# Gated linear attention in a fused transformer kernel: two decay levels written as blocks over the first score products, and a new order of the work around them

## The reference, cut to what matters

```python
def step(state, inp):            # gla_chunk_scan, once forward, once on flipped tokens
    qc, kc, vc, gc = inp
    cum = jnp.cumsum(gc, axis=2)
    o_inter = jnp.einsum('bhcd,bhde->bhce', qc * jnp.exp(cum), state)
    rel = cum[:, :, :, None, :] - cum[:, :, None, :, :]
    decay = jnp.exp(jnp.where(mask[:, :, None], rel, -jnp.inf))
    attn = jnp.einsum('bhid,bhjd,bhijd->bhij', qc, kc, decay)
    o = o_inter + jnp.einsum('bhij,bhje->bhie', attn, vc)
...
k = rmsnorm(dk.reshape(b, n, DIFF_HEADS, 2, DIFF_DH)..., k_norm_g)   # diff_qkv
```

## Time and profile before

| | |
|---|---|
| Median of three runs | 1724.3 us (1721.74 to 1725.12) |
| The profiled execution | 1722.09 us, span 1720.5 us |
| Mean granted TensorE clock | 0.961 |
| TensorE matmuls busy | 1586.4 us |
| VectorE / ScalarE / GpSimd busy | 929.1 / 720.2 / 153.1 us |

### The profile page before, as it was taken

How to read it: one execution, slowest core, us unless ns; L and a number is a source line. 1 busy time by engine, 2 the same in 40 slices (tenths; PEclk the granted TensorE clock), 3 DMA queues, 4 the chain that set the end, 5 groups by cost and what they waited for, 6 DMA issues and landing times.

```text
span 1720.5 us, 18791 instructions
## 1 busy us (share of the span) xinstructions
PE 1586.4 (92%) x7442; PEld 1250.1 (73%) x7442; DVE 929.1 (54%) x1399; ACT 720.2 (42%) x1116; POOL 153.1 (9%) x106
## 2 busy tenths in 40 slices
PE   8998889798989999999899899998876999999995
PEld 1776767587778888888678677786664788888884
DVE  3656568885654433333625655365646666246644
ACT  4443346466342222222433667454445444234432
POOL 0100122442000000000100010120211100000001
PEclk9999989789999999999899999999988999999998
DMA  9431101200534233222222222232202132233231
GB/s 363 178 140 42 45 25 62 74 1 1 203 115 147 76 98 121 98 77 92 78 98 67 68 70 72 67 118 85 77 10 98 60 100 75 97 109 98 83 97 53
DMA packets 47949, 156.57 MB, mean 91 GB/s; under 512 B 5588, under 2 KB 10324, under 8 KB 47351
## 3 DMA queue, kind: packets, MB, share of 16 engines
q1 hardware_dynamic: 47280, 152.00, 26.0%
q10 hardware_dynamic: 582, 3.38, 0.6%
HBM read 153.26 MB, written 2.10 MB: 90 GB/s over the span
## 4 chain that ended last, share of the span: by engine, by line
PE 73%; DVE 13%; ACT 8%; issue 4%; POOL 1%; DMA 1%; ACTq 0%; DVEq 0%; SPq 0%
PE pall L1979 17%; PE pall L1981 17%; PE pall L1980 17%; ACT whi L547 2%; DVE wlo L1193 2%; PE pall L2013 2%; PE pall L2421 1%; PE pall L2014 1%; PE pall L2015 1%; PE pall L2423 1%; PE pall L2422 1%; PE pall L1997 1%; PE pall L1998 1%; PE pall L1999 1%; PE pall L2055 1%
## 5 line engine op out<-in xcount | busy, mean ns | idle before, releaser
L1193 DVE TENSOR_TENSOR wlo<-raw,whi 128x1024 fp32r<-128x1024 f32 (+2 forms) x261 | 290.2, 1113 | 326.6 <-ACT whi L547 326.5
L547 ACT ACTIVATE whi<-raw 128x1024 fp32r<-128x1024 f32 (+2 forms) x263 | 246.5, 939 | 161.4 <-PE pall L1981 122.0
L1979 PE MATMUL pall<-h5h,whi 128*128 128x512 f32 x320 | 125.2, 391 | 1.9 <-DVE wlo L1193 1.9
L1981 PE MATMUL pall<-h5h,wlo 128*128 128x512 f32 x320 | 125.2, 391 | 0.0
L1980 PE MATMUL pall<-h5l,whi 128*128 128x512 f32 x320 | 125.0, 391 | 0.0
L1979 PE MATMUL pall<-h2h,whi 128*128 128x512 f32 x320 | 124.5, 389 | 0.0
L1980 PE MATMUL pall<-h2l,whi 128*128 128x512 f32 x320 | 124.5, 389 | 0.0
L1981 PE MATMUL pall<-h2h,wlo 128*128 128x512 f32 x320 | 124.5, 389 | 0.0
L1144 ACT ACTIVATE tmp<-pall,vec 128x512 f32<-128x512 f32 x44 | 34.1, 779 | 92.5 <-PE pall L1981 88.2
L1979 PEld LDWEIGHTS pall<-h5h,whi 128*128 128x128 f32 x320 | 60.5, 189 | 15.0 <-issue 2.3
L1980 PEld LDWEIGHTS pall<-h5l,whi 128*128 128x128 f32 x320 | 60.5, 189 | 12.6
(11 more groups left out here) (447 smaller groups left out, 3641.9 us busy)
## 6 DMA issues: line engine op xcount, KB each, us to landing
raw<-in_weights SPq DMA_DIRECT2D x204, 512.0 KB, 3.4
mraw<-in_wmod SPq DMA_DIRECT2D x32, 512.0 KB, 4.6
mod<-in_weights SPq DMA_DIRECT2D x16, 512.0 KB, 12.5
raw<-in_weights SPq DMA_DIRECT2D x25, 256.0 KB, 2.6
raw<-in_weights SPq DMA_DIRECT2D x32, 192.0 KB, 2.3
xT<-in_x SPq DMA_DIRECT2D x1, 2048.0 KB, 17.1
xT<-in_x ACTq DMA_DIRECT2D x1, 2048.0 KB, 8.1
out_y<-xT SPq DMA_DIRECT2D x8, 256.0 KB, 2.1
```

The source lines that it names most:

```text
L547: e.activation(whi[j % 3][:, 0:cols(j)], raw[j % 4][:, 0:cols(j)], ACT.Copy).then_inc(s.hi, 1)
L1193: e.tensor_tensor(wlo[j % 3][:, 0:n], raw[j % 4][:, 0:n], f(whi[j % 3][:, 0:n]), ALU.subtract).then_inc(s.lo_v, 1)
L1979: e.matmul(o_, a[:, kk, :], xh(k), start=(k == 0), stop=False)
L1981: mm = e.matmul(o_, b[:, kk, :], xh(k), start=False, stop=(k == nk - 1))
```

## The change

Levels 1 and 2 (`MG = 2`) no longer have steps of their own. Their products are made only on the off-diagonal blocks (64x64 and 32x32) and written straight over the step-0 product in banks 6 and 7; since ACT doubles that product on its way out, queries and keys of these levels carry a factor sqrt(0.5) each. The steps become `item`s, six for each pair of heads, at new places (`ITEM_AT`). Gates come by pair of heads, and the gaps of levels 1 and 2 and the decayed keys' gap are made inside the loop over `gv`. `key_sums` moves from tile 6 to tile 2 of the next `dk` product (and tile 2 of `gr0`), the item there from tile 2 to tile 5. `heads_out(1)` moves to tile 7 of `dq2`, head 2's sum to tile 7 of `dq3`, head 3's sum before the last query's; their banks are 6 and 7 instead of 3.

```diff
-JOBS = (... "h0", "h1", "dq0", "dq1", "dq2", "dq3", "h2", "h3", ...)
+JOBS = (... "h0", "h1", "dq0", "dq1", "dq2", "h2", "h3", "dq3", ...)
+        MG = 2
+        NI = 8 - MG
+        ITEM_AT = {1: 0, 2: 1, 3: 2, 4: 3, 5: 4, 6: 5, 8: 6, 9: 7, 10: 8, 11: 9, 12: 10, 13: 11}
+        GAPS_AT = {0: (2,), 1: (3,), 2: (4,), 3: (5,), 4: (6,), 6: (7, 8), 7: (9,), 8: (10,), 9: (11,), 10: (12,), 11: (13,)}
+        KEYS_AT = {0: (0, 1), 1: (2,), 2: (3,), 3: (4,), 4: (5,), 5: (6,), 7: (7, 8), 8: (9,), 9: (10,), ...}
# ACT, loop over gv
                 gate(i)
+                if i >= 2:
+                    key_decay(i - 2)
+                    decays(i - 2)
# DVE, loop over gv
                 gate(i)
+                if 1 <= i < 3:
+                    key_gap(i - 1)
+                    level_gaps(i - 1)
# DVE, level_keys
+                if lev <= MG:
+                    e.scalar_tensor_tensor(QKl[t][:, :, :], Db[t][:, :, :], math.sqrt(0.5), qk[:, hp, :, :], ALU.mult,
+                                           ALU.mult).then_inc(s.lmul, 1)
# PE
-            def level(n):
+            def item(j):
...
+                if k == 0:
+                    w.wait_ge(s.lmul, 7 * hp + MG)
+                    for lev in range(1, MG + 1):
+                        t = level_at(7 * hp + lev - 1)[2]
+                        b = 64 >> (lev - 1)
+                        for c in range(0, 512, 2 * b):
+                            for kc_, qc in ((c, c + b), (c + b, c)):
+                                for sub in range(2):
+                                    p = slice(64 * sub, 64 * sub + 64)
+                                    to = bank(6 + sub)[kc_ % 128:kc_ % 128 + b, qc:qc + b]
+                                    mm = e.matmul(to, QKl[t][p, 1, kc_:kc_ + b], QKl[t][p, 0, qc:qc + b], start=True,
+                                                  stop=True)
# PE, dk, gr, dq
-                     between={2: lambda: level(4 + i), 6: lambda: key_sums(i - 1) if i else state(3)})
+                     between={2: lambda: key_sums(i - 1) if i else state(3), 5: lambda: item_at(4 + i)})
-                     between={2: lambda: level(8 + i), 6: lambda: beside_r(i)})
+                     between={5 if i == 0 else 2: lambda: item_at(8 + i), 2 if i == 0 else 6: lambda: beside_r(i)})
-                     between={2: lambda: level(12 + i), 6: lambda: query_sums(i - 1) if i else None})
+                between = {2: lambda: item_at(12 + i)}
+                if i:
+                    between[5 if i == 1 else 3] = lambda: query_sums(i - 1)
+                if i == 2:
+                    between[7] = lambda: heads_out(1)
+                if i == 3:
+                    between[7] = lambda: sums("h2", s.hosq, 3, ones, tmp[1], 6)
+            sums("h3", s.hosq, 4, ones, tmp[1], 7)
             query_sums(3)
-            heads_out(1)
-            sums("h2", s.hosq, 3, ones, tmp[1], 3)
-            sums("h3", s.hosq, 4, ones, tmp[1], 3)
```

More of the change, by code:

```diff
@@ L177, in __getitem__ @@
         return self.value[name]
-JOBS = (["ctx", "x"] + [f"dk{i}{p}" for i in range(4) for p in "xc"] + ["h0", "h1", "dq0", "dq1", "dq2", "dq3",
-        "h2", "h3", "d0", "d1", "d2", "d3", "norm2", "mixpre", "mem", "mixpost", "xapre", "xapost", "ffnpre", "ffnpost"])
+JOBS = (["ctx", "x"] + [f"dk{i}{p}" for i in range(4) for p in "xc"] + ["h0", "h1", "dq0", "dq1", "dq2", "h2",
+        "h3", "dq3", "d0", "d1", "d2", "d3", "norm2", "mixpre", "mem", "mixpost", "xapre", "xapost", "ffnpre", "ffnpost"])
 def build(nc, ap, out):
@@ L1405, in _ @@
             for n in range(4):
-                level(n, ("dv", 2 * n))
+                if n:
+                    for i in GAPS_AT[n]:
+                        level_gaps(i)
+                lo(J[("dv", 2 * n)] + 2)
+                if n == 0:
+                    level_keys(0)
+                    level_keys(1)
+                    level_gaps(2)
+                if n >= 2:
+                    level_keys(n + 1)
+                    item_scores(ITEM_AT[n])
                 if n:
@@ L1437, in _ @@
             for i in range(4):
-                level(4 + i, ("dk", i, 0))
+                n = 4 + i
                 if i == 0:
                     state(3)
+                if n == 4:
+                    level_gaps(6)
+                if n == 6:
+                    level_gaps(7)
+                    level_gaps(8)
+                lo(J[("dk", i, 0)] + 2)
+                for k in KEYS_AT.get(n, ()):
+                    level_keys(k)
+                if n == 7:
+                    level_gaps(9)
+                if i == 0:
                     query_gap(0)
@@ L1459, in _ @@
             for i in range(4):
-                level(8 + i, ("gr", i, 0))
+                n = 8 + i
+                for k in GAPS_AT[n]:
+                    level_gaps(k)
+                lo(J[("gr", i, 0)] + 2)
                 if i == 0:
                     key_norm(3)
+                    level_keys(9)
+                else:
+                    level_keys(n + 1)
+                    item_scores(ITEM_AT[n])
                 if i == 1:
@@ L1484, in key_parts @@
                     e.tensor_tensor(Ql[i][:, :], Qd[:, h, :], f(Qh[i][:, :]), ALU.subtract).then_inc(s.kql, 1)
+            for i in range(4):
+                n = 12 + i
+                lo(J[("dq", i, 0)] + 2)
+                if i == 0:
+                    level_keys(13)
+                if n in ITEM_AT:
+                    item_scores(ITEM_AT[n])
+                if i == 0:
+                    query_gap(1)
+                    out_norm(1)
+                else:
+                    query_norm(i - 1)
             key_parts(0, 0)
+            out_norm(2)
             key_parts(0, 1)
-            out_norm(2)
             out_norm(3)
+            query_norm(3)
             def diff_max(n, c):
```

245 lines of the change are left out of this document (119 added, 126 removed).

## The result

The changed kernel takes 1709.4 us (median of 4 runs, 1708.6 to 1710.6; the kernel before beside it 1723.9). The ratio of the two is 0.9918, with a 95% interval from 0.9901 to 0.9935 (written [0.9901, 0.9935] from here on). A second measurement (experiment 12) gave 0.9921. I had said 1707, range 1700 to 1717.

A forecast was written before the change was run, and what follows sets the result against it. The prediction took TensorE's work plus its waits, 124 to 332 us, as the bound. Its terms, -10.9 - 8.0 + 1.7 = -17.2 us against 1722.1, gave 1704.9; with 2.2 for the median, 1707, range 1700 to 1717.

The forecast's parts named there:

- a. First turning: First turning of keys: no step stands before it, so it starts at about 131.4 instead of 135.5, gain 4.1 us.
- b. The blocks: Item 0's 96 more narrow matmuls cost 2.9 us an item, bounds 1.4 and 5.3.
- Rivals 1 and 4: Item-0 blocks: first, 0.059 us a matmul, time 1710, chance 0.14; second, about 0.17, time 1731, chance 0.05.
- c. Values: Values' products, turning of n = 2: -4.1 + 2.9 + 1.1 = -0.1 us, its wait growing from 0.8 to about 1.9.
- d. Key norms: From `key_sums(0)`, 5.4 us earlier, through DVE and ACT's 48.4 us chain to `item(7)` in `gr1`: gain 10.9 us.
- f. Queries and last heads: From `dq0` to the differential products: 6.6 us earlier on TensorE, 9.5 at DVE's first maximum, taken as 8.0.
- g. Clock: Waits at the second turning and before `item(7)` may each drop the clock for 1.7 us; one taken, +1.7.
- rival 1: Narrow products are dear: no starts closer than 0.059 us, gain 14.2, time 1710, chance 0.14.
- Rival 2: The end, queries to differential stage, gives little: 2 to 3 us instead of 8, time 1712 to 1713, chance 0.13.
- Rival 3: Key norm chain is longer, 1.5 us more at each norm: time 1711 to 1712, chance 0.10.

The follow-up runs named there:

- experiment 12: The changed kernel itself measured once more, nothing altered: 1709.4 us, ratio 0.9921.
- experiment 6: Kernel before with the new order of key norms and gates by pair; no blocks, sixteen steps, queries as before: 1699.7 us, ratio 0.9866.
- experiment 8: Changed kernel with queries and last heads as before, item 7's product ahead of key norm 3, `level_keys(2)` ahead of `state(0)`: 1700.2 us, ratio 0.9866.
- experiment 1: Kernel before with only the new order of key norms: 1704.2 us, ratio 0.9897.
- experiment 5: Changed kernel with one line moved, VectorE's product for item 7 before the norm of key 3: 1702.6 us, ratio 0.9883.
- experiment 9: Kernel of experiment 8 with key roots 1 and 2 before the exponentials of levels 7 to 9, level 9's gaps behind norm 2: 1703.1 us, ratio 0.9882.
- experiment 2: Changed kernel with queries and last two heads in the order of before: 1706.05 us, ratio 0.9899.
- Experiment 10: Kernel of experiment 8 with the sums of the last two heads in banks 6 and 7, not both in bank 3: 1699.7 us, ratio 0.9863.

## Why the prediction was right

The time was right because errors of both signs met, so in part by luck. By its own steps:

*a. First turning:* forecast 4.1 us earlier; 14.7 to 10.6 in the table. Right, and the clock dropped there as said. That it stays up after 1.92 us of waiting (experiment 6) I had not seen.

*b. The blocks:* 1.3 us an item, not 2.9, and at my lower bound (96 x 0.014 is 1.34, which I had rounded to 1.4). Mis-sized was the price of a matmul: 0.0154 us for 64 columns and 0.0090 for 32, where I had 0.028 and 0.025; the changes of shape take 0.27, near my 0.4. Two steps failed: "two instructions each have to be issued, so I take 0.025 for those", and the price by stationary columns itself, whose 0.028 and 0.014 are both too dear. Rivals 1 and 4 fall. The Trainium skill, "TensorE: Matmul & The Clock Gate" (Part 1, "Wait — 56ns, not 53.3ns?"), has starts no closer than about 25 ns, and some 62 ns with software decoding; the trace agrees with neither, as here they are 15.4 and 9.0 ns apart.

*c. Values:* -0.1 at turning 2 was forecast, -1.0 measured (160.36 - 120.87 = 39.5 us before, 38.5 after). Two errors met: the blocks are 1.6 cheaper, and TensorE waits 1.14 us before item 1, since `level_keys(2)` stands behind `state(0)`, which I had priced for the turning and not for the item. Turning 2 waited 0.81, not 1.9. With it moved turning 2 is 1.4 us earlier (experiment 8).

*d. Key norms:* `item(7)` 10.9 us earlier was forecast, 12.0 measured, with no wait before `dk2` and 1.4, 1.25 and 4.24 before `dk3`, `gr0` and item 7 where I had 2, 2 and 3. Right in size and place, the single waits by luck in part (6.9 us together, 7 forecast). The chain from `key_sums(0)` to item 7 took 48.4 us (68.9 to 117.4), as I had it; the 1.1 more lie ahead of it, as `key_sums(0)` stands 6.6 us earlier and not 5.4. But what I took for the gain of the change was what it left of a larger one: the new order alone gives 18.7 at that place (experiment 1), with the chain at 40.6 us. Of the 7.9 that it is longer in the changed kernel, 3.6 go with the one line before norm 3 (experiment 5). The waits of 1.39 and 1.25 and the 1.3 of item 6's blocks make up most of the other 4.3; that they come from the gaps and exponentials of merged levels between the norms is argued, since the edit that took both waits away brought one of 3.36 (experiment 9).

*f. Queries and last heads:* this step failed. "Gain 6.6 where TensorE starts its differential products", 9.5 at VectorE's first maximum, 8.0 in all: measured from the item in `dq0` on, 4.1 at the first differential product, 6.1 at the first maximum and 5.4 at the end of the stretch. Mis-sized is the way to head 3's sum, 36.9 us from that item where I had 34.5: `heads_out(1)` starts at 20.7 and not 19.1, head 2's sum stands at 32.3 behind `dq3` and not 30.1. The wait of 3 before head 3's sum is 2.96 in the trace, and the 7.8 us for two roots and norms behind it are 7.9. And the part that I ascribed to the new order is a loss: with the old order the first differential product comes 3.1 us sooner behind that item, the first maximum 1.2 (experiment 2). What shortens `dq` are the two steps that it no longer holds, the last of which had waited 2.93 us in the kernel before (303.75 above), and the clock behind that wait. What I never worked out is the old order with two steps fewer.

*g. Clock:* +1.7 forecast, 2.3 measured behind item 7, none at turning 2.

The sum in the stretch: -12.0 + 2.3 - 5.4 = -15.1, and 15.2 were measured. It was -17.2 in the forecast: (f) is 2.6 short and the clock 0.6 dearer, while item 7 is 1.1 earlier. In time rival 1 (1710) is nearest to the 1709.4, but its reason is refuted. Rival 2 names the right place, the end, with 2 to 3 us where 5.4 were measured. Rival 3 falls: the chain was as long as forecast.

Open stays whether the merging of levels is worth it at all. With it (experiments 8, 10) and without it (6) the totals are equal. Without, the step in `gr1` is 7.9 us earlier than in 8, and 5.7 of these come back in `dq`; 2.2 are left at the first maximum and 2.0 at the end of the stretch. Experiment 10's edit, which gains 2.0 there, was not made on the kernel of 6.

## What to carry to other kernels

When a change has several parts, price what each is worth with the others undone: here one part alone was worth the whole, and one was a small loss that hid behind steps saved by another. When an instruction is put between two links of a chain that crosses engines, look at what the in-order queue holds behind it on every engine: three waits of this case (1.1, 4.2 and 3.4 us) are a ready or nearly ready operation behind one that waited. And a comparison from a fixed mark ahead of the change to marks behind it shows where a difference arises, when totals can't tell 2 us. Set the last mark close behind the change: what lies further on differed here by up to 2.6 us between kernels in which that part is the same work.

## What the runs showed of the hardware

- Narrow float32 matmuls in alternating halves of the rows start 15.4 ns apart (64 rows, 64 stationary and 64 streamed columns) and 9.0 ns apart (32 and 32), 13.6 in the mean with the changes of shape, 192 in a row. Of a set of 384, TensorE stands after 210 for 2.65 and then 1.11 us, or after 233 for 2.17 and then 2.22, with 128 matmuls between the two stands each time, and goes on 1.4 to 1.5 us after a 16 KB packet of the instruction queue has landed. The Trainium skill, "Runtime: NRT & Kernel Launch" (Instruction fetch mechanics), says that fetching instructions hides behind their issue; for such sets it doesn't.
- The granted clock doesn't go by the length of a wait alone. After 1.88 us of waiting it was 0.62 over 4.5 us in the kernel before, after 1.92 it was 1.00 in experiment 6, after 1.39 and 1.25 1.00 in the changed kernel, after 3.33 and 4.24 0.64 and 0.61. Before the last step in `dq` the same wait stands in two kernels: after 2.93 it was 0.57 in the kernel before, after 2.91 1.00 in experiment 1.
